# Feed forward's down projection as seven block products in place of eight

## The reference, cut to what matters

```
h2 = rmsnorm(x, g_mlp[l])
x = x + jnp.square(jax.nn.relu(h2 @ w_ff1[l])) @ w_ff2[l]
ple_gate = jax.nn.sigmoid(rmsnorm(x, g_ple[l]) @ w_ple_gate[l])
```

## Time and profile before

| what | value |
|---|---|
| median of 3 executions | 3534.4 us (3533.42 to 3536.12) |
| the profiled execution | 3542.31 us |
| its span, first to last instruction | 3540.5 us |
| PE, DVE, ACT, POOL busy | 96%, 64%, 44%, 23% of the span |
| mean granted TensorE clock | 0.985 |

### The profile page before, as it was taken

One profiled execution on the slowest core, in us unless ns is written; L12 is line 12 of the kernel. 1 busy time (PEld: TensorE's weight loads), 2 busy tenths in 40 slices (PEclk: granted clock), 3 DMA queues, 4 the chain that ended last, 5 costly groups with the idle time before them and its releaser, 6 DMA issues.

```text
span 3540.5 us, 43930 instructions
## 1 busy us (share of the span) xinstructions
PE 3409.3 (96%) x17289; PEld 2810.1 (79%) x17289; DVE 2259.2 (64%) x2915; ACT 1575.3 (44%) x1946; POOL 798.8 (23%) x396
## 2 busy tenths in 40 slices
PE   7999999999999999999999999999897999999998
PEld 6667767667878878888888877777775899999997
DVE  4334445645457675666765854545756999999998
ACT  4344443234322353332113433433545677777776
POOL 3111111111222345544431221111222111101112
PEclk9999999999999999999999999999898999999999
DMA  5111113223465323336542241232633999999998
GB/s 201 49 48 54 66 54 103 78 95 124 159 223 179 105 85 119 116 137 220 201 162 71 81 157 65 83 117 92 195 125 148 382 380 379 388 384 386 380 380 310
DMA packets 131725, 626.75 MB, mean 177 GB/s; under 512 B 14849, under 2 KB 15241, under 8 KB 106690
## 3 DMA queue, kind: packets, MB, share of 16 engines
q1 hardware_dynamic: 126626, 606.12, 46.1%
q0 software_dynamic: 4752, 17.30, 1.8%
q10 hardware_dynamic: 144, 0.52, 0.0%
HBM read 520.67 MB, written 103.19 MB: 176 GB/s over the span
## 4 chain that ended last, share of the span: by engine, by line
PE 55%; DVE 4%; ACT 1%; issue 1%; DMA 1%; POOL 1%; POOLq 0%; DVEq 0%; SPq 0%; ACTq 0%
PE bank L268 8%; PE bank L270 7%; PE bank L269 7%; PE bank L3866 5%; PE bank L3867 5%; PE bank L3865 5%; PE bank L2123 3%; PE bank L2124 3%; PE bank L2125 3%; PE bank L3881 2%; PE bank L3882 2%; PE bank L3883 2%; DVE gqJ L2972 1%; PE bank L3852 1%; PE bank L2846 1%
## 5 line engine op out<-in xcount | busy, mean ns | idle before, releaser
L257 POOL TENSOR_TENSOR WL<-WR,WH 128x1024 fp32r<-128x1024 f32 (+1 forms) x177 | 400.7, 2264 | 1728.1 <-ACT WH L249 1725.0
L268 PE MATMUL bank<-XH,WH 128*128 128x512 f32 x1584 | 639.7, 404 | 10.1 <-ACT stg L553 5.1
L270 PE MATMUL bank<-XH,WL 128*128 128x512 f32 x1584 | 620.1, 391 | 0.0
L269 PE MATMUL bank<-XL,WH 128*128 128x512 f32 x1584 | 619.8, 391 | 0.0
L249 ACT ACTIVATE WH<-WR 128x1024 fp32r<-128x1024 f32 (+1 forms) x177 | 173.4, 980 | 516.4 <-PE bank L270 511.3
L3801 DVE TENSOR_TENSOR EL<-ER,EH 128x2816 fp32r<-128x2816 f32 x120 | 371.4, 3101 | 2.8 <-ACT EH L3796 2.8
L268 PEld LDWEIGHTS bank<-XH,WH 128*128 128x128 f32 x1584 | 298.7, 189 | 88.7 <-issue 15.9
L3796 ACT ACTIVATE EH<-ER 128x2816 fp32r<-128x2816 f32 x120 | 307.5, 2564 | 117.6 <-PE bank L3867 81.3
L269 PEld LDWEIGHTS bank<-XL,WH 128*128 128x128 f32 x1584 | 299.1, 189 | 64.9 <-issue 5.0
L270 PEld LDWEIGHTS bank<-XH,WL 128*128 128x128 f32 x1584 | 298.7, 189 | 63.4
L3865 PE MATMUL bank<-EH,WH 128*128 128x352 f32 x1024 | 336.6, 329 | 2.0 <-DVE WL L3989 2.0
(11 more groups left out here) (655 smaller groups left out, 6966.5 us busy)
## 6 DMA issues: line engine op xcount, KB each, us to landing
ER<-in_wu_dram SPq DMA_DIRECT2D x48, 1408.0 KB, 8.7
ER<-in_wd_dram SPq DMA_DIRECT2D x40, 1408.0 KB, 11.4
WR<-in_w_in_dram SPq DMA_DIRECT2D x89, 512.0 KB, 4.5
ER<-in_wg_dram SPq DMA_DIRECT2D x32, 1408.0 KB, 8.8
WR<-in_w_ff_dram SPq DMA_DIRECT2D x64, 512.0 KB, 4.7
aq<-in_w_ada_dram SPq DMA_DIRECT2D x48, 512.0 KB, 3.5
res<-in_wg_dram SPq DMA_DIRECT2D x16, 1408.0 KB, 8.5
res<-in_wu_dram SPq DMA_DIRECT2D x16, 1408.0 KB, 8.5
```

The costliest lines, as they stand in the source:

```text
L257: e.tensor_tensor(lo, raw, hi.bitcast(F32), ALU.subtract).then_inc(*w_lo.up("w_lo", n))
L268: e.matmul(bank[bk][:, 0:b - a], whi, xhi, start=k == 0, stop=False)
L269: e.matmul(bank[bk][:, 0:b - a], whi, xlo, start=False, stop=False)
L270: mm = e.matmul(bank[bk][:, 0:b - a], wlo, xhi, start=False, stop=k == K - 1)
```

## The change

The down projection becomes 16 more units (16 to 31) of the same seven-product form, in one loop with the up units. The depth is cut into four chunks c of 1024; unit n = 16 + 4c + p makes output tiles 2p and 2p+1 of chunk c. For this the seven activation factors of each chunk are formed behind the up units: DVE subtracts squared outputs (`up_factor`: T1, T3, T2, T4), SP stores seven 128x512 blocks per up unit (four before), and up units take tiles n%4 and n%4+4 of a group of eight, so that units 4c to 4c+3 make chunk c. At a change of chunk each factor is reloaded (one 128x2048 DMA of 1 MB), split by ACT and by DVE (POOL for factor 3), into the place where it lay, once the last unit of the chunk before has done that product.

```
+    D_f = scratch("D_f", [4, 7, 128, 4 * 512])
+    def down_load(e, c, i):
+        e.wait_ge(*on("up.mm", 15 + 4 * c, i))
+        for n in range(4 * c, 4 * c + 4):
+            e.wait_ge(*on("h.out", n, i))
+        e.dma_start(factor4(i, False), D_f[c, i].rearrange("p (a b) -> p a b", b=512)).then_inc(...)
+    def down_hi(e, c, i):
+        e.wait_ge(*on("f.in", c, i))
+        for s in range(2):
+            e.activation(factor4(i, True, s), factor4(i, False, s), AF.Copy)...
+    def down_lo(e, by, c, i):
+        for s in range(2):
+            e.wait_ge(*on("f.hi", c, i, s))
+            e.tensor_tensor(factor4_lo(i, s), factor4(i, False, s), factor4(i, True, s).bitcast(F32), ALU.subtract)...
+    def dn_bank(n, i):
+        return (7 * n + i) % 4
+    def unit_pe(e, n):
+        for i in range(7):
+            bk = up_bank(n, i) if n < 16 else dn_bank(n, i)
+            ... wait: the bank's last reader, "up.lo" of the weight; at a chunk's first unit "f.lo" (c, i, half)
+            for k in range(4):
+                3 matmuls, as in an up unit
+            if n == 17 and i == 0:
+                ada_pe(e)
-        for t in range(32):            # 48 matmuls a tile
-            ...
```

DVE's order in a down unit (`down_dve`; `r(t, h)` is a 128x512 piece of the residual, p2 to p7 are banks):

```
+        if first_: down_lo(e, V, c, 2); down_lo(e, V, c, 4)
+        for i in ada_of(n, 0): ada_dve(e, i)
+        e.tensor_tensor(r(0, 0), r(0, 0), p2, ALU.add)          # waits up.mm(n, 1)
+        e.tensor_tensor(r(0, 1), r(0, 1), p5, ALU.add)          # waits up.mm(n, 2)
+        e.tensor_tensor(r(1, 1), r(1, 1), p5, ALU.add)
+        up_sum(e, n + 1, 2)
+        if first_: down_lo(e, V, c, 5)
+        for i in ada_of(n, 1): ada_dve(e, i)
+        e.tensor_tensor(keep2, p6, keep1, ALU.add)              # waits up.mm(n, 3)
+        if first_: down_lo(e, V, c, 6)
+        up_sum(e, n + 1, 3)
+        if last: down_lo(e, V, c + 1, 0)
+        e.tensor_tensor(r(0, 1), r(0, 1), p3, ALU.add)          # waits up.mm(n, 4)
+        up_sum(e, n + 1, 4); up_sum(e, n + 1, 5)
+        if last: down_lo(e, V, c + 1, 1)
+        for i in ada_of(n, 2): ada_dve(e, i)
+        e.tensor_tensor(keep3, p7, keep2, ALU.add)              # waits up.mm(n, 5)
+        e.tensor_tensor(r(1, 0), r(1, 0), p4, ALU.subtract)     # waits up.mm(n, 6)
+    ADA = {17: (0, 2, 1), 18: (2, 1, 1), 19: (2, 1, 0), 20: (0, 1, 0), 21: (2, 2, 1), 22: (2, 2, 2), 23: (2, 2, 1),
+           24: (0, 2, 1), 25: (2, 2, 2), 26: (2, 2, 2), 27: (2, 2, 2)}      # w_ada tiles per slot
     def ada_dve(e, a):
-        for i in range(2):
+        for i in range(2 if a < 16 else 1):
```

The kept sums (keep1 to keep3) are added to the residual by POOL, four 128x512 additions a unit, among its seven weight splits:

```
+        for n in range(16, 31):
+            if first_of_chunk(n): down_lo(e, ff_pool, c, 3)
+            up_lo(e, n + 1, 0); up_lo(e, n + 1, 1); first_back(e, n)
+            for i in (6, 2, 3): up_lo(e, n + 1, i)
+            second_back(e, n)
+            up_lo(e, n + 1, 4); up_lo(e, n + 1, 5); third_back(e, n)
```

More of the change, by code:

```diff
@@ L2022, in first_factors_dve @@
         factor_lo(e, T2, 1)
[L2025 to L2035, removed]
-        else:
[L2037 to L2040, removed]
@@ L2054, in down_at @@
[L2054 to L2066, removed]
+    keep1, keep2, keep3, junk = first_kept, c_slots[C12], c_slots[C21], acq[:, 0:512]
@@ new lines, in program, with ada_of, ada_raw, ada_end @@
+    ADA = {17: (0, 2, 1), 18: (2, 1, 1), 19: (2, 1, 0), 20: (0, 1, 0), 21: (2, 2, 1), 22: (2, 2, 2), 23: (2, 2, 1),
+           24: (0, 2, 1), 25: (2, 2, 2), 26: (2, 2, 2), 27: (2, 2, 2)}
+    def ada_of(n, s):
+        if n not in ADA:
+            return ()
+        a = sum(sum(ADA[m]) for m in range(17, n)) + sum(ADA[n][:s])
+        return range(a, a + ADA[n][s])
+    def ada_raw(a):
+        return stg[:, a % 2 * T:a % 2 * T + T]
+    def ada_end(a):
+        return ("ada.ev", a, 1 if a < 16 else 0)
@@ L2078, in ff_sp @@
         for t in (0, 2):
             for i in (4, 5):
-                e.wait_ge(*on("up.sum", 15, i))
+                e.wait_ge(*on("up.sum", 31, i))
             for i in (0, 1, 6):
[L2082 to L2097, removed]
-        for t in range(32):
[L2099 to L2104, removed]
-    def ada_load(e, m):
-        e.wait_ge(*(on("ada.ev", m - 2, 1) if m > 1 else on("ada.bc", 1, 1)))
-        e.dma_start((ac2, acq)[m % 2], I["w_ada"][m]).then_inc(*d_ada[m % 2].up("ada", m))
+                e.wait_ge(*on("up.lo", 31, i))
@@ new lines, in ff_sp, with ada_next, ada_pe @@
+            w_load(e, N_PLE + t)
+        e.wait_ge(*on("up.mm", 31, 2))
+        w_load(e, N_PLE + 1)
+    def ada_next(e, n, s):
+        for a in ada_of(n, s):
+            if a + 2 < 48:
+                ada_load(e, a + 2)
+    def ada_load(e, m):
+        e.wait_ge(*(on(*ada_end(m - 2)) if m > 1 else on("ada.bc", 1, 1)))
+        e.dma_start(ada_raw(m), I["w_ada"][m]).then_inc(*d_ada[m % 2].up("ada", m))
+    def ada_pe(e):
+        for i in range(2):
+            for h in range(2):
+                e.wait_ge(*on("ada.diag", i))
+                e.wait_ge(*on.bank(4 + 2 * i + h, *ada_end(15 if i else 47)))
+                for k in range(4):
+                    o = (4 * h + k) * 128
+                    mm = e.matmul(bank[4 + 2 * i + h][:, k * 128:k * 128 + 128], ones, ada_raw(i)[:, o:o + 128],
+                                  start=True, stop=True)
+                mm.then_inc(*ff_pe.up("ada.bc", i, h))
@@ new lines, in dn_bank @@
+    def dn_bank(n, i):
+        return (7 * n + i) % 4
+    DN_READ = ("dn.p1", "dn.p2", "dn.p5", "dn.p6", "dn.p3", "dn.p7", "dn.p4")
+    def unit_pe(e, n):
+        for i in range(7):
+            bk = up_bank(n, i) if n < 16 else dn_bank(n, i)
+            if n < 16:
+                e.wait_ge(*on.bank(bk, "up.free", n, i))
+            else:
+                e.wait_ge(*on.bank(bk, DN_READ[i], n))
+            e.wait_ge(*on("up.lo", n, i))
+            for k in range(4):
+                if n == 0:
+                    e.wait_ge(*on("ff.plo", i, k))
+                if first_of_chunk(n) and k % 2 == 0:
+                    e.wait_ge(*on("f.lo", n // 4 - 4, i, k // 2))
+                whi, wlo = (w(n, i)[:, k * 128:k * 128 + 128] for w in (UH, UL))
+                xhi, xlo = FH(i, k), FL(i, k)
+                e.matmul(bank[bk][:, :], whi, xhi, start=k == 0, stop=False)
+                e.matmul(bank[bk][:, :], whi, xlo, start=False, stop=False)
+                mm = e.matmul(bank[bk][:, :], wlo, xhi, start=False, stop=k == 3)
+            mm.then_inc(*ff_pe.up("up.mm", n, i))
+            if n == 0 and i == 4:
+                e.wait_ge(*on("wo.sum"))
+                rstd_pe(e, acq, T, (4, 0), ("ff",))
+            if n == 17 and i == 0:
+                ada_pe(e)
@@ L2112, in ff_pe_ @@
             on.holder[bk] = "ff.plo", i, k
[L2113 to L2132, removed]
-                for i in range(2):
[L2134 to L2146, removed]
+        for n in range(32):
+            unit_pe(e, n)
     def up_keep(e, n):
-        e.wait_ge(*(on("up.ev", n - 1, 3) if n else on("w_used", N_FF - 1)))
+        e.wait_ge(*(on("up.ev", n - 1, 3) if n else on("w_used", N_PLE - 1)))
         e.wait_ge(*on("up.mm", n, 0))
@@ L2164, in ff_act_ @@
         rstd_act(e, rN, 1024, T, (4, 0), ("ff",))
-        for n in range(15):
+        for n in range(16):
             up_keep(e, n)
@@ new lines, in ff_act_ @@
+            up_square(e, n, 3)
+        for n in range(16, 28):
+            c = n // 4 - 4
+            first_, last = first_of_chunk(n), last_of_chunk(n)
+            keep_first(e, n)
+            up_hi(e, n + 1, 0)
+            if first_:
+                down_hi(e, c, 5)
+            up_hi(e, n + 1, 1)
+            if first_:
+                down_hi(e, c, 6)
+            up_hi(e, n + 1, 6)
+            up_hi(e, n + 1, 2)
+            if last:
+                down_hi(e, c + 1, 0)
+            up_hi(e, n + 1, 3)
+            if last:
+                down_hi(e, c + 1, 1)
+            up_hi(e, n + 1, 4)
+            if last:
+                down_hi(e, c + 1, 2)
+            up_hi(e, n + 1, 5)
+            if last:
+                down_hi(e, c + 1, 3)
+                down_hi(e, c + 1, 4)
```

424 lines of the change are left out of this document (312 added, 112 removed).

## The result

| | before | after |
|---|---|---|
| median, same chip | 3535.3 us (3533.4 to 3539.0, 4 runs) | 3586.0 us (3583.4 to 3587.0, 4 runs) |
| profiled execution, span | 3542.3, 3540.5 | 3587.0, 3585.1 |

The ratio is 1.0137 (95% interval 1.0124 to 1.015): 51 us slower, where I had forecast 15 and a range up to 3582. The two spans differ by 44.6 us; the rest is that the profiled execution of before lay 7 us over its median, that of after 1.

The account below looks back on a forecast made before the run. DVE, with its turns with POOL, was taken to bound units 16 to 28: down +14.0 and gate +1.3 give +15 us on the median of 3534.4, so 3549, range 3507 to 3582.

Parts of the forecast that it names:

- PE's 43.5 us: Down units: 192 fewer matmuls at 0.227 save 43.5 us; were PE never late, down would take 304.6.
- DVE the bound from unit 18 on: Units 16 to 28: DVE's clean work is 249 us against PE's 247.5, with nothing to spare.
- One sign: Units 16 to 28: PE below 85% busy with DVE above 95% would show the forecast right.
- The lock: Units 16 to 28: DVE and POOL take turns when both read two SBUF tiles; losses sum to 59 us.
- The rival with less lock: Same DVE chain, losing 22 us in place of 59: 3512; at twice that rate 3534; chance 30%.
- Units 16 and 17: DVE's cost with losses was put at 28.0 us for unit 16 and 17.9 for unit 17.
- DVE enters unit 16 about 4 us behind PE: Entry to unit 16: two chunk 0 splits in unit 15 and two factors after the last output (4 x 0.6).
- the diagonals (3.2): Unit 16: DVE's making of the ada diagonals, priced at 3.2 us.
- The gate: Handover from down to gate: PE loses 2.8 us where it lost 1.5 before, +1.3.
- The sum: DVE is done with unit 28 at 314.6 us; down takes 369.1 in place of 355.1, +14.0.
- Late reload: Chunk changes: at 209 GB/s reloads need 53 us, 13 too many at three changes: 3588; late reload or clock 18%.
- The clock: Stalls also cost clock: four are 14 us, partly under DVE's time; late reload or clock 18%.

Follow-up runs that it names:

- the last experiment: Changed kernel with diagonals on ACT, unit 31's squares moved, factor 3 split by DVE, later chunks' DVE splits from PSUM, w_ada reductions over 32 columns: 3516.9 us, ratio 0.9941.
- the one other order tried at unit 16: Against the changed kernel, DVE in unit 15 reads the last two banks before unit 16's sums 4 and 5, T1 and splits of factors 1, 2, 4: 3588.9 us.

## Why the prediction was right in kind and too small in size

- **PE's 43.5 us.** Right: an undisturbed unit lasts 19.04, and all were given back. The 304.6 leaves out PE's spread of the ada vectors, 3.7 at the full clock, which stood within the 355.1 before.
- **DVE the bound from unit 18 on.** Right. Counted on DVE, from its last addition of unit 17 to that of unit 28 (1647.9 to 1913.3), these units were priced at 264.7 and took 265.5, none off by more than 2.8. PE's own lengths differ more (28: 35.7 against 26.1), since DVE's lateness in a chunk's last unit stops PE in the next one. That the sum is so close is partly luck: DVE waited 12.2 us for `w_ada` tiles, which I had not priced, and units 18 to 21, 24 and 28 cost less than I had put. One sign did not come: in units 16 to 28 PE was busy for 82%, below my 85, but DVE for 90%, not above 95.
- **The lock.** Right in size for the splits and sums: 53 us measured beside an estimate of 59. Turns, not one side to the end: 10.77 for four halves with POOL's instructions between. The rival with less lock fell by that.
- **Units 16 and 17: the step that failed.** "DVE enters unit 16 about 4 us behind PE", and the prices 28.0 and 17.9 for units 16 and 17, had DVE through unit 17 at 49.9 us after PE's start of unit 16. It was through at 71.8, **+21.9**. It entered 13.9 us behind (+9.9): its work for unit 15 met POOL's split of factor 3, and a split took 4.01 (2.35 alone), a relu 2.61 and a subtraction 2.84 (0.69 each in the run with factor 3 on DVE). PE's second product of unit 16 waited 9.24 for the bank read after them. Unit 16 took DVE 30.7 (+2.7), with "the diagonals (3.2)" at 9.41. Unit 17 took it 27.2 (+9.3): I had added up DVE's queue without asking who waits for its last entry, and PE's spread, which I had put at nothing, stands in order in front of six products: DVE stood idle for 9, behind the spread and the two products after it. The run with ACT's diagonals took 9.5 off PE's 64.9 for the two units. DVE, POOL and PE at the entry to unit 16 (PE starts it at 1576.05, DVE's list for it at 1589.96):

```profile
1576.71 4.01 DVE L2108 TENSOR_TENSOR YL<-YLf,YH 128x1024 fp32r<-128x1024 f32 x2 [0.45 <-ACT YH L2103]
...
1582.15 2.61 DVE L2356 SCALAR_TENSOR_TENSOR XLf<-XLf,stg 128x512 f32<-128x512 f32 x1
1584.68 2.84 DVE L1916 TENSOR_TENSOR stg<-XLf,XHf 128x512 f32<-128x512 f32 x1
...
1589.96 5.70 DVE L2108 TENSOR_TENSOR YL<-YLf,YH 128x1024 fp32r<-128x1024 f32 x4
...
1581.86 5.10 POOL L2108 TENSOR_TENSOR XL<-XLf,XH 128x1024 fp32r<-128x1024 f32 x2
...
1588.17 0.80 PE L2215 MATMUL bank<-YH,WH 128*128 128x512 f32 x1 [9.24 <-DVE XLf L2397]
```

- **The gate.** "I take 2.8 lost, +1.3" was mis-sized: +10.9. I counted the steps that PE could do meanwhile, and not that sixteen `next_lo` are stretched by POOL's last add-backs and weight splits (5.0 more of waits), nor the clock that fell with the waits (5.9).
- **The sum.** The 21.9 to the end of unit 17 and 0.8 from there to unit 28 are the 22.7 by which down exceeds its forecast (36.7 against 14.0). With 9.6 for the gate it is 32; with the later stages 3 shorter, 29 of the 36 us between forecast and measured change. The rest is the profiled executions: that of before lay 7 us over its median, that of after 1.
- **Late reload.** Not for the factors. The DMA issues of the changed kernel's down units (columns as in the earlier trace rows) have 1 MB factors land after 7.5 and 9.7 us in the median, not over 20; DVE waited 0.4 us for ACT's copies of them, and the last experiment takes the same bytes faster. What DVE did wait for, 12.2 us, are the `w_ada` tiles loaded between them (last line, columns as in the earlier trace rows):

```profile
YLf<-D_f SPq DMA_DIRECT2D x13, 1024.0 KB, 7.5
XLf<-D_f SPq DMA_DIRECT2D x11, 1024.0 KB, 9.7
...
L2510 DVE CUSTOM_DVE_ANT_0 aq<-stg,bank,par 128x512 f32<-128x512 f32 x64 | 47.8, 748 | 18.6 <-DMA stg<-in_w_ada_dram 12.2 <-DVE WR L1954 0.2
```

  4.0 of the 12.2 fall in unit 23 and 3.3 in unit 27, just before a change of chunk. No run took these waits away, so how much of them reached PE is open.

  The clock, which I had put beside it, did fall in the long units (0.84 to 0.90): 22.5 us of PE's time, 17 of them in units 20, 24 and 28, where DVE was busy throughout anyway. How much of it counted was not separated. At the gate it counted, with 5.9.

## What to carry to other kernels

Before work is taken from the bounding engine, add up the next engine's work with the time it loses to the engine it shares with: here 249 us of work against 247.5 of PE left no room, and the one other order tried at unit 16 gained nothing. A term from the sum of a queue is not enough where a stage begins or ends; there, follow the last entry to the one who waits for it. Moving work from POOL to DVE can be free when DVE would have stood behind it.

## What the runs showed of the hardware that I had not expected

- Sixteen `tensor_scalar` of 128x128 on DVE took 9.41 us in the changed kernel and 8.76 with the other order at unit 16, beside a full POOL queue (3.22 before), with POOL at 1.27 an instruction: the waiting was all DVE's. DVE's splits with a PSUM operand were not held: 36 of them took 1.21 each beside POOL.
- Five waits of together 6.3 us, none longer than 2.5, went with a loss of 10.9 at the gate: after the second of them matmuls went from 0.39 to 0.63 us, and the granted clock was 0.50 over ten us.
